# Second projection pass placed behind the first head's scores, and seven of sixteen cache copies issued at the turns of tiles

## What is computed

```
z = x @ w_in                       # 1024 -> 2560 columns: q, k, v, GLU value a, GLU gate g
att = mixture of three dilated windows (128,1) (512,4) (2048,16) over q, k, v, 8 heads x 64
conv = swish(LayerNorm(depthwise causal conv, 31 taps, of a * sigmoid(g)))
x1 = LayerNorm(ALPHA * x + concat(att, conv) @ w_out)
q = x1 @ w_query                   # 8 heads x 2 x 128
per head: top 16 of 128 key scores on each side, top 16 of the 256 sums -> 16 experts, softmax gate
peer = sum over 128 experts of gate * gelu(x1 . u[e]) * v[e]     # u, v: 16384 x 1024 each
y = LayerNorm(ALPHA * x1 + peer)
```

## Time and profile before

| | us |
|---|---|
| median of three runs | 3468.59 |
| the profiled execution | 3467.86 |
| its span | 3466.1 |
| VectorE busy | 2707.0 (78%) |
| TensorE busy | 2575.0 (74%) |
| GpSimd busy | 1260.2 (36%) |
| ScalarE busy | 713.7 (21%) |

### The profile page before, as it was taken

One profiled execution on the slowest core, in us unless ns is written; L12 is line 12 of the kernel. 1 busy time (PEld: TensorE's weight loads), 2 busy tenths in 40 slices (PEclk: granted clock), 3 DMA queues, 4 the chain that ended last, 5 costly groups with the idle time before them and its releaser, 6 DMA issues.

```text
span 3466.1 us, 39995 instructions
## 1 busy us (share of the span) xinstructions
PE 2575.0 (74%) x14040; PEld 1167.4 (34%) x14040; DVE 2707.0 (78%) x7309; ACT 713.7 (21%) x1562; POOL 1260.2 (36%) x1092
## 2 busy tenths in 40 slices
PE   7974578767766876787678767876787666789876
PEld 5533345322332333233324332433243322234321
DVE  5178888789799969996999699969996984346855
ACT  2210132013201420152015201520152002122110
POOL 0012222225444443444435444444444332224342
PEclk8987789888888888889889888988898888889999
DMA  9999999989999999999999999999999999999998
GB/s 339 367 398 373 352 395 358 417 338 396 421 411 367 421 421 421 389 421 421 421 385 418 421 421 393 417 421 421 397 416 421 421 411 422 418 420 397 419 388 333
DMA packets 218457, 1386.73 MB, mean 400 GB/s; under 512 B 28424, under 2 KB 39176, under 8 KB 67336
## 3 DMA queue, kind: packets, MB, share of 16 engines
q0 software_dynamic: 156672, 1140.92, 80.4%
q1 hardware_dynamic: 41040, 141.81, 10.8%
q10 hardware_dynamic: 20544, 101.45, 7.3%
HBM read 1370.99 MB, written 80.04 MB: 419 GB/s over the span
## 4 chain that ended last, share of the span: by engine, by line
DVE 39%; DMA 29%; PE 20%; issue 9%; ACT 2%; POOL 1%; SPq 0%; POOLq 0%; ACTq 0%; DVEq 0%
DMA t<-in_expert_uv,t 28%; DVE t L1099 12%; PE psum L1477 9%; DVE t L966 4%; PE psum L1379 3%; DVE psum L1126 3%; PE psum L1420 2%; DVE t L1111 2%; PE psum L1301 2%; DVE t L1047 2%; DVE t L1045 2%; DMA t<-glu_scratch 2%; DVE t L1048 1%; DVE t L1046 1%; DVE t L990 1%
## 5 line engine op out<-in xcount | busy, mean ns | idle before, releaser
L645 POOL DMA_INDIRECT t<-in_expert_uv,t x1088 | 1260.0, 1158 | 2172.0 <-PE psum L1473 829.5
L1477 PE MATMUL psum<-t,t 64*64 64x512 f32 x4896 | 1365.4, 697 | 640.6 <-DVE t L1111 640.1
L1099 DVE CUSTOM_DVE_ANT_0 t<-t,t 128x1024 f32<-128x1024 f32 x1088 | 1322.0, 1221 | 476.3 <-DMA t<-in_expert_uv,t 466.3
L1477 PEld LDWEIGHTS psum<-t,t 64*64 64x64 f32 x4896 | 347.2, 150 | 1472.2 <-DVE t L1111 864.9
L1473 PE MATMUL psum<-t,t 64*64 64x512 f32 x2496 | 762.1, 740 | 0.0
L805 ACT ACTIVATE t<-t 128x2 f32<-128x2 f32 x544 | 110.8, 204 | 1846.4 <-DVE t L1099 1844.9
L1420 PEld LDWEIGHTS psum<-t,t 128*128 128x128 f32 x2304 | 276.7, 200 | 72.2 <-issue 64.8
L1420 PE MATMUL psum<-t,t 128*128 128x128 f32 (+1 forms) x2304 | 288.1, 286 | 2.6 <-ACT t L767 2.6
L1301 PE MATMUL psum<-t,t 128*128 128x128 f32 (+2 forms) x768 | 256.0, 494 | 26.2 <-DMA t<-in_xT 25.6
L966 DVE SCALAR_TENSOR_TENSOR t<-t,t,t 128x128 f32<-128x128 f32 x840 | 238.2, 345 | 0.0
L1301 PEld LDWEIGHTS psum<-t,t 128*128 128x128 f32 x768 | 132.0, 202 | 138.2 <-issue 111.3
(11 more groups left out here) (142 smaller groups left out, 2054.7 us busy)
## 6 DMA issues: line engine op xcount, KB each, us to landing
t<-in_wq_t ACTq DMA_DIRECT2D x65, 1024.0 KB, 9.8
out<-in_cache_k_win SPq DMA_DIRECT2D x8, 4080.0 KB, 41.7
out<-in_cache_v_win SPq DMA_DIRECT2D x8, 4080.0 KB, 45.8
t<-in_w_in_t ACTq DMA_DIRECT2D x44, 512.0 KB, 8.0
t<-in_kc_t SPq DMA_DIRECT2D x8, 2560.0 KB, 18.7
t<-in_vc_t SPq DMA_DIRECT2D x8, 2560.0 KB, 13.8
t<-in_expert_uv,t POOLq DMA_INDIRECT x1088, 14.2
t<-in_w_v_t ACTq DMA_DIRECT2D x6, 1024.0 KB, 10.5
```

The lines of the kernel that those rows point to most:

```text
L645: pool.indirect_dma_start(ring[:, r, :], None, I["expert_uv"], bass.IndirectOffsetOnAxis(ap=idn[t % 2][:, s:s + 1], axis=0)).then_inc(land ...
L1099: dve.tensor_tensor_reduce(out=ring[:, r, 0:D], in0=x1[t % 2][:, :], in1=ring[:, r, 0:D], scale=1.0, scalar=0.0, op0=ALU.mult, op1=ALU.add ...
L1477: last = pe.matmul(MAIN[t][half][NS * a:NS * a + NS, :], zt[NS * a:NS * a + NS, k % Z_RING, j, :], vv[NS * a:NS * a + NS, :], start=(c == ...
```

## The change

The second pass's units go from places 43 to 123 (two of them at 43, then about one each 3.5 places) to places 66 to 123 (one each 2.5 places), behind the first head's key scores at place 65. The product of value and gate of the second pass is taken 7 places after its unit in place of 4, and its store 10 places after in place of 7; for the third pass both stay as they were. Of the copies, 0 to 4 are issued as before, copies 5 and 6 at `a_route` 1 and 3, copies 7 to 13 in turn right behind `front_loads(m)` for m = 1 to 7, and copies 14 and 15 behind copies 7 and 8, when four heads of tile 1 and of tile 2 have their scores reduced (`sm_done` 12 and 20).

```diff
-UNIT_PLACE = [[4 * (10 + j * 21 // 24) + 3 for j in range(24)], [4 * GROUPS + 1 + j * 8 // 3 for j in range(24)]]
+UNIT_PLACE = [[66 + j * 60 // 24 for j in range(24)], [4 * GROUPS + 1 + j * 8 // 3 for j in range(24)]]
-EVAC_LAG, GATE_LAG, STORE_LAG = 2, 4, 7
-GATE_PLACE = [[UNIT_PLACE[p][2 * i + 1] for i in range(CT)] for p in range(2)]
+EVAC_LAG, GATE_LAG, STORE_LAG = 2, (7, 4), 3
+GATE_PLACE = [[UNIT_PLACE[p][2 * i + 1] + GATE_LAG[p] for i in range(CT)] for p in range(2)]
...
-            for i in range(PH):
+            for i in range(5):
                 if i:
                     sp.wait_ge(sm_done, i)
...
-            def cache_copies():
-                for i in (2, 5):
-                    sp.wait_ge(sm_done, PH + i)
-                    copy_cache(PH + 3 + (i + 1) // 3)
-                for i in (1, 4):
-                    sp.wait_ge(a_q, PH + i)
-                    copy_cache(PH + 6 + (i + 1) // 3)
...
-            for i in range(4):
-                sp.wait_ge(a_route, 2 * i if i else 1)
-                copy_cache(PH + i)
+            for i in range(2):
+                sp.wait_ge(a_route, 2 * i + 1)
+                copy_cache(5 + i)
             projected_loads()
             for n in range(TILES + 1):
                 m = n + 1
...
                 if m < TILES:
                     front_loads(m)
+                if m < PT:
+                    copy_cache(6 + m)
+                if m in (1, 2):
+                    sp.wait_ge(sm_done, PH * m + 4)
+                    copy_cache(13 + m)
...
-                if m == 1:
-                    cache_copies()
...
-                        for p, j in gates_at(place(n, q) - GATE_LAG):
+                        for p, j in gates_at(place(n, q)):
                             gated(p, j)
```

## The result

The change makes the kernel slower: 3491.97 us median (3488.08 to 3493.41, 6 runs) against 3470.43 for the kernel before in the same comparison, a ratio of 1.0061 (95% interval 1.0047 to 1.0076). The prediction was 3458, with a range up to 3480. The profiled execution after took 3493.41 us.

The account below looks back on a forecast made before the run. The kernel was taken as bound by fixed DMA traffic plus DMA idle time. Stage -1 -52, stage 0 -5, stages 2 to 6 +34, stage 1 +15 and better flow -2 make -10: 3467.86 becomes 3458 us, range 3440 to 3480.

Parts of the forecast that it names:

- The sum: Whole kernel: terms -52, -5, +34 and +15 give -8 us, with -2 for better flow -10, so 3458 us.
- the turns of stages 2 to 6: One copy each behind the q and GLU loads: 10 us less a hidden hole, +6.8 a stage, +34 for five.
- stage 0: Loses copies 12 to 15, gets 7 and 14: -3 us in its first part, -2 in its second, -5 together.
- the seven heads: Rest of stage -1 after the first routing: 231.3 us becomes 216, as 190 without waits plus 26.
- What bounds the kernel: Whole kernel: a fixed amount of DMA traffic plus the time in which the DMA engines have nothing to do.
- The 23 us a copy: Counter-price from the Trainium skill's 358 GB/s HBM limit: 13 us more a copy, some 80 us loss; the trace does not agree.
- The first routing at 134 us: Start of kernel: without eight second-pass units a 52 us chain from 82.4 ends at 134, not 170.3, 36 us earlier.
- 4 us because the second head's scores now stand behind three units: Seven heads of stage -1: part of the 26 us added to 190 for the heads, priced at 4 us.
- That it no longer stands in the queue gives 0: Stage 0: the 12th copy no longer ahead of the third pass's tokens in the queue is worth 0 us.
- Stage 1: Gets two copies, +20 us, less 5 us for holes in its first part: +15 us.
- Rival A, which ended at 3493,: TensorE becomes the bound of stage -1: units at 9.4 us, -52 becomes -17, time 3493 us; chance 0.15.
- Rival B: Everything is a swap: turns cost +70 in place of +49, or heads take 227; time 3468, no change; chance 0.25.

Follow-up runs that it names:

- e3: The changed kernel without copies 9 to 13, the five at the turns of stages 2 to 6: 3446.21 us, ratio 0.9917.
- e6: The changed kernel with one second-pass unit in place of three between the first and second head's key scores: 3493.7 us, ratio 1.0064.
- e10: The kernel before with copy 15 moved from stage 0's second part to when all but the last dot are done: 3469.99 us, ratio 0.9997.
- e7: The changed kernel with copies 7 and 14 asked for at sm_done 10 and 13, none behind the loads at stage 0's turn: 3497.73 us, ratio 1.008.
- e9: The changed kernel with the second pass's units at places 66 to 117 in place of 66 to 123: 3487.11 us, ratio 1.0054.
- e2: The kernel before with SyncE's queue (the copies) of the change and the units where they were: 3523.02 us, ratio 1.0142.
- e4: The changed kernel without copies 5 and 6, the two in the seven heads of stage -1: 3484.92 us, ratio 1.0028.
- e8: The changed kernel with copies 5 to 15 re-placed, laid into stretches where its DMA engines are idle: 3449.94 us, ratio 0.9939.

## Why the prediction was wrong

The sum had -8 us for the span, and +25.5 came. Three of its terms make up 32 of these 33.5 us, and all three were counted too low: the turns of stages 2 to 6 (+34 became +48.2), stage 0 (-5 became +4.7) and the seven heads (216 became 224.2).

- **What bounds the kernel** stood: the same bytes plus holes. Every experiment is read by it. The 23 us a copy that the prediction set beside its own price did not come (9.2 by e3).
- **The first routing at 134 us** came at 133.9. The 52 us chain, and the claim that the DMA engines have no hole up to there (share 1.03), held.
- **The seven heads**, 216 forecast, took 224.2. The term that failed is "4 us because the second head's scores now stand behind three units": the four waits for ScalarE are 18.0 us. I counted the units in front of the second head's scores, and followed neither TensorE's order further, to the third head's queries behind a fourth unit, nor ScalarE's, where the copy of these queries stands ahead of the first gates' exponential. e6, with two of the units taken out of this head, ends the waits and takes it from 47.6 us to 38.6. The waits for gathers were less than I had counted, 13.1 us in place of 22 with the first one. 190 + 18.0 + 13.1 is 221; most of the other 3 us is VectorE's own work, 185.22 us in place of 182.66.
- **Stage 0**, -5 forecast, +4.7. The second part held: two copies fewer and 117.3 us as before, where I had taken off 2 us; e10 shows it once more. In the first part I had priced only the copies. "That it no longer stands in the queue gives 0" looked at what stood ahead of the tokens' load, and not at when it is asked for: the denser units end nearer to the turn, 14 us ahead in place of 19, the tokens take the way of the GLU rows, and VectorE waits 9.1 us in place of 2.0 (e7 and e9). e2, with the old placement, had 0.8 us of that wait and a stage 0 of 341.2 us, -3: that is the copies' own part.
- **The turns**, 6.8 a copy and +34 in all, were +48.2, 8.2 to 11.1 a stage, and 9.2 a copy by e3. The step that failed is the overlap: the sum took 10 us less the whole hole of 3.3, as if a stage could then end 3.3 us sooner. The windows at the turn of 1429.4 us of the changed kernel, against the earlier trace rows:

```profile
1430.00:1440.00 10.00, 8.85 (x34) 2.76 (x36) 8.57 (x22) 4.46 (x8) 2.60 (x2) 0.83 1.03 388
1440.00:1450.00 10.00, 10.00 (x42) 3.25 (x38) 7.42 (x22) 0.20 (x1) 5.33 (x5) 1.00 1.02 386
1450.00:1460.00 10.00, 6.96 (x33) 2.01 (x32) 7.02 (x17) 1.49 (x2) 3.74 (x3) 1.00 1.02 425
```

The hole of 0.76 is filled, but at a full share only 386 to 388 GB/s flow for 20 us in place of 421: 20 x (1 - 387/421) = 1.6 us are lost again beside it. Which of the three transfers beside each other (GLU rows, copy, gathers) lowers the rate was not tried. Nor does what is won at the turn last to the end of the stage. Stages 2 to 6 whole, first before, then after:

```profile
1098.80:2835.70 1736.90, 1305.22 (x7784) 563.21 (x7784) 1499.58 (x4190) 395.49 (x835) 758.95 (x640) 0.87 1.00 413
```

```profile
1074.20:2859.30 1785.10, 1315.27 (x7784) 565.01 (x7784) 1505.53 (x4190) 395.40 (x835) 758.07 (x640) 0.87 1.01 414
```

Had the holes been won, the rate of these stages would have risen to 417 GB/s. It is 413 and then 414 GB/s, so five copies (20.9 MB) cost nearly what they take at that rate, 50 us. In the 30 us behind each turn the changed kernel moves more, 390 GB/s on average in place of 363, which is 2.0 us a turn; in the rest of the stage it moves less than at the full 421 GB/s by 1.7 us more than before. What opens these later holes was not tried.

- **Stage 1**, +15 forecast, came at +14.4.
- **Rival A, which ended at 3493,** was right on the number by luck. Its way was slow units in six heads of seven, and the granted clock rose from 0.78 to 0.89 of 2.4 GHz, as the argument against it had said; most of the loss lies in stages 1 to 6. But for the first of the seven heads it had the right engine. The prediction named a wait of VectorE for `a_sc`, the copied scores, as a sign of it: that is the wait of 3.9 us at L1039, and TensorE is busy for 47.60 us of this head's 47.60, at a clock of 1.00. It is the number of units that bounds the head, and not their slowness.
- **Rival B** had two branches, each priced nearly right: +70 for the seven copies (+62.6 came), or 227 us for the heads (224.2 came). They came together. Its sum was wrong: with +70 in place of +49 the forecast of 3458 becomes 3479 and not 3468, and with the heads' 11 us as well 3490, next to the 3492 measured.
- **The sum.** Three terms were wrong by 8, 10 and 14 us, all on one side, and a small difference of two large sums, -57 and +49, takes its sign from such errors. The bounds for the seven copies (+35 to +70) were written down, and the measured +62.6 lies within them, but the range up to 3480 has room for only one term at its bad end.

## What to carry to other kernels

Where the DMA engines are full, background copies cost nearly their whole time, even where they fill a hole at the start of a stage, so the question for each is not when it is convenient but where the engines are idle and nobody waits for a gather; look for a stretch whose DMA share can fall without its length changing. A move that frees one stretch and a move that empties it are worth judging together, since here -11 and +52 made +21.5 and not +41. And when units are packed more closely on one in-order engine, follow everything that now stands behind them on it, the engine that copies it out, and the load that the last unit releases.

## What the runs showed that I had not expected

A copy from DRAM to DRAM, 4080 KB, cost 9.2 to 10 us of time beside gathers (e3). In the seven heads the first two cost 3.6 us each (e4) and the next two 8 us each (e8 against the change), and in two places a copy cost nothing that could be measured (e10). The first of the seven heads took 47.6 us in seven kernels with the same placement, whatever flowed beside it, and 38.6 us with two units fewer in it. A 316 KB load of GLU rows was waited for 9.1 us when a 1792 KB load in the same queue had been asked for 14 us ahead of the turn, 2.0 us with 19 us ahead, and not at all with 30 us (e9).
